# Index scores and softmax logits of a two-layer trunk: a head's high and low query parts stacked over 128 rows

## The reference, cut to what matters

```python
proj = x @ w_in + b_in            # 1024 -> q_a|k_a|v_a|g_a|q_b|k_b|v_b|g_b|q_i|k_i|w_i|r_a|r_b
head_scores = relu(einsum('bthi,bsi->bths', q_idx, k_idx))        # 8 heads of 64, one key head
index_score = einsum('bth,bths->bts', w_idx, head_scores)         # -inf where not admissible
_, sel = lax.top_k(index_score, n_select)                         # 128 keys (prompt), 80 (sample)
logits = einsum('bthd,btkd->bhtk', q, k_sel) * ATT_SCALE + bias   # 8 heads of 64, one key head
p = softmax(logits); y_b = einsum('bhtk,btkd->bthd', p, v_sel)
```

## Time and profile before

| | us |
|---|---|
| median of 3 runs | 1003.15 (1001.43 to 1004.92) |
| profiled execution | 1001.84, its span 1000.0 |
| PE busy | 970.6 (97%) |
| PE weight loads busy | 889.9 (89%) |
| DVE busy | 775.6 (78%) |
| ACT busy | 526.7 (53%) |
| POOL busy | 555.8 (56%) |
| chain that ended last | PE 77%, DVE 14%, ACT 3%, issue 3%, POOL 1% |

### The profile page before, as it was taken

The page is one execution under the profiler, slowest core; times in us unless marked ns, Lnnn a source line. Parts: engine busy times, 40 slices in busy tenths (PEclk is TensorE's granted clock), DMA queues, the critical chain, the costliest instruction groups (busy, mean ns, idle before and its releaser), DMA issues.

```text
span 1000.0 us, 18578 instructions
## 1 busy us (share of the span) xinstructions
PE 970.6 (97%) x7192; PEld 889.9 (89%) x7192; DVE 775.6 (78%) x1417; ACT 526.7 (53%) x936; POOL 555.8 (56%) x466
## 2 busy tenths in 40 slices
PE   6999998999999999999999999989999999999996
PEld 5889997788899999998888899877888999999985
DVE  7479998769997966559864899977898978656447
ACT  5564346668867454343235633476698474344320
POOL 2535555636665597676434366554465647677550
PEclk9999999999999999999999999999999999999999
DMA  7612452101112231265343135301111122231712
GB/s 218 215 48 95 160 164 90 33 13 43 54 36 82 86 111 60 85 214 185 97 161 111 44 97 167 125 16 43 44 44 43 43 85 85 86 126 43 270 46 95
DMA packets 71164, 96.51 MB, mean 97 GB/s; under 512 B 4499, under 2 KB 62341, under 8 KB 70437
## 3 DMA queue, kind: packets, MB, share of 16 engines
q1 hardware_dynamic: 67124, 83.74, 25.9%
q0 software_dynamic: 3776, 11.50, 3.2%
q10 hardware_dynamic: 176, 0.07, 0.0%
HBM read 82.09 MB, written 14.79 MB: 97 GB/s over the span
## 4 chain that ended last, share of the span: by engine, by line
PE 77%; DVE 14%; ACT 3%; issue 3%; POOL 1%; DMA 0%; DVEq 0%; ACTq 0%; POOLq 0%
PE ps L1053 21%; PE ps L676 15%; PE ps L986 10%; PE ps L1107 9%; DVE attn L1779 4%; DVE top L1776 3%; PE ps L700 3%; DVE attn L1752 3%; PE ps L901 3%; PE ps L922 2%; PE ps L961 2%; PE ps L940 2%; PE ps L724 2%; PE ps L880 2%; PE ps L1099 1%
## 5 line engine op out<-in xcount | busy, mean ns | idle before, releaser
L2200 POOL TENSOR_TENSOR w_lo<-raw,w_hi 128x512 fp32r<-128x512 f32 x71 | 97.1, 1368 | 228.8 <-ACT w_hi L1154 228.6
L676 PE MATMUL ps<-xT_hi,w_hi 128*128 128x288 f32 x480 | 143.1, 298 | 0.0
L676 PE MATMUL ps<-xT_hi,w_lo 128*128 128x288 f32 x480 | 141.4, 295 | 0.0
L676 PE MATMUL ps<-xT_lo,w_hi 128*128 128x288 f32 x480 | 141.4, 295 | 0.0
L2317 POOL TENSOR_TENSOR w_lo<-raw,w_hi 128x512 fp32r<-128x512 f32 x76 | 106.7, 1414 | 47.0 <-ACT w_hi L1511 46.6
L2201 POOL TENSOR_TENSOR w_lo<-raw,w_hi 128x512 fp32r<-128x512 f32 x71 | 103.9, 1463 | 0.0
L676 PEld LDWEIGHTS ps<-xT_hi,w_hi 128*128 128x128 f32 x480 | 90.1, 188 | 1.2 <-issue 0.6
L676 PEld LDWEIGHTS ps<-xT_lo,w_hi 128*128 128x128 f32 x480 | 90.1, 188 | 0.0
L676 PEld LDWEIGHTS ps<-xT_hi,w_lo 128*128 128x128 f32 x480 | 90.0, 188 | 0.0
L1511 ACT ACTIVATE w_hi<-raw 128x512 fp32r<-128x512 f32 x76 | 47.5, 629 | 80.6 <-PE ps L1053 49.9
L2317 POOL TENSOR_TENSOR w_lo<-w_sums,w_hi 128x512 fp32r<-128x512 f32 x48 | 73.1, 1532 | 24.9 <-ACT w_hi L1511 24.4
(11 more groups left out here) (282 smaller groups left out, 3178.8 us busy)
## 6 DMA issues: line engine op xcount, KB each, us to landing
raw<-in_w_in SPq DMA_DIRECT2D x44, 1024.0 KB, 5.2
raw<-in_w_out SPq DMA_DIRECT2D x8, 1024.0 KB, 5.3
x_kept<-x_nat SPq DMA_DIRECT2D x2, 2560.0 KB, 10.3
x_nat<-x_kept SPq DMA_DIRECT2D x2, 2560.0 KB, 10.4
raw<-in_w_proj_a SPq DMA_DIRECT2D x8, 512.0 KB, 3.5
raw<-in_w_proj_b SPq DMA_DIRECT2D x8, 512.0 KB, 4.5
x_nat<-in_x_prompt SPq DMA_DIRECT2D x4, 512.0 KB, 5.4
out<-stage POOLq DMA_DIRECT2D x8, 256.0 KB, 5.3
```

Of the source, the lines that this page charges most:

```text
L676: last = mm(out, a, b[:, HALF * half:HALF * (half + 1)], start=(k == 0 and i == 0), stop=(k == n - 1 and i == 2))
L2200: g.tensor_tensor(lo[:, 0:half, :], src[:, 0:half, :], hi[:, 0:half, :].bitcast(f32), ALU.subtract)
```

## The change: what it does

q_hi and q_lo become one array q_both[128, 2, 4, TOK]. For head hh of a pair, q_both[:, hh, m] holds the high part in the partitions where the head's queries lie and the low part in the other 64. One matmul over all 128 partitions by the high keys gives high x high plus low x high; then a matmul over the head's own 64 partitions by the low keys adds high x low. A call issues four matmuls, full, full, half, half, in place of six halves. ACT makes the high parts in two instructions of 64 partitions, and DVE and POOL the low parts in two each, which cross the partition halves. POOL also waits for the low part of a unit's weights, and for each of its two query parts in turn, before it goes on.

```diff
-        with nc.sbuf_tensor("q_hi", [128, 4, TOK], f32r) as q_hi, nc.sbuf_tensor("q_lo", [128, 4, TOK], f32r) as q_lo:
+        with nc.sbuf_tensor("q_both", [128, 2, 4, TOK], f32r) as q_both:
             pass
...
                     if s >= 4:
                         pe.wait_ge(s_relu, L * NH * N_IDX + s - 2)
-                    for i, (q, k) in enumerate(((q_hi, ki_hi), (q_hi, ki_lo), (q_lo, ki_hi))):
-                        for hh in range(2):
-                            p = slice(64 * hh, 64 * hh + 64)
-                            last = mm(ps[0:n, 4 + (s + hh) % 4, 0:nk], q[p, h // 2, t0:t0 + n], k[p, k0:k0 + nk],
-                                      start=(i == 0), stop=(i == 2))
-                            if i == 2:
-                                last.then_inc(s_is, 1)
+                    for hh in range(2):
+                        mm(ps[0:n, 4 + (s + hh) % 4, 0:nk], q_both[:, hh, h // 2, t0:t0 + n], ki_hi[:, k0:k0 + nk],
+                           start=True, stop=False, skip_group_check=True)
+                    for hh in range(2):
+                        p = slice(64 * hh, 64 * hh + 64)
+                        mm(ps[0:n, 4 + (s + hh) % 4, 0:nk], q_both[p, hh, h // 2, t0:t0 + n], ki_lo[p, k0:k0 + nk],
+                           start=False, stop=True, skip_group_check=True).then_inc(s_is, 1)
...
# logits(p): the same with kb_hi, kb_lo and s_lg; its stage waits for s_qblo at L * 8 + 8
...
-                    act_f(q_hi[:, m, at:TOK], qy[:, m if kind == "QI" else 4 + m, at:TOK], ACT.Copy).then_inc(s_qhi, 1)
+                    for hh in range(2):
+                        p = slice(64 * hh, 64 * hh + 64)
+                        last = act_f(q_both[p, hh, m, at:TOK], qy[p, m if kind == "QI" else 4 + m, at:TOK], ACT.Copy)
+                    last.then_inc(s_qhi, 1)
...
-                    v.tensor_tensor(q_lo[:, m, QI_AT:TOK], qy[:, m, QI_AT:TOK], q_hi[:, m, QI_AT:TOK].bitcast(f32),
-                                    ALU.subtract).then_inc(s_qilo, 1)
+                    for hh in range(2):
+                        p, other = slice(64 * hh, 64 * hh + 64), slice(64 - 64 * hh, 128 - 64 * hh)
+                        done = v.tensor_tensor(q_both[other, hh, m, QI_AT:TOK], qy[p, m, QI_AT:TOK],
+                                               q_both[p, hh, m, QI_AT:TOK].bitcast(f32), ALU.subtract)
+                    done.then_inc(s_qilo, 1)
...
-                    g.tensor_tensor(q_lo[:, m, :], qy[:, 4 + m, :], q_hi[:, m, :].bitcast(f32), ALU.subtract).then_inc(s_qblo, 1)
+                    pool.wait_ge(s_lo, L * T0 + u + 4)
+                    for hh in range(2):
+                        p, other = slice(64 * hh, 64 * hh + 64), slice(64 - 64 * hh, 128 - 64 * hh)
+                        pool.wait_ge(s_qblo, L * 8 + 2 * m + hh)
+                        g.tensor_tensor(q_both[other, hh, m, :], qy[p, 4 + m, :],
+                                        q_both[p, hh, m, :].bitcast(f32), ALU.subtract).then_inc(s_qblo, 1)
+                    pool.wait_ge(s_qblo, L * 8 + 2 * m + 2)
```

More of the change, by code:

```diff
@@ L834, in _ @@
                 pe.wait_ge(s_kblo, L * 2 + 2)
-                pe.wait_ge(s_qblo, L * 4 + 4)
+                pe.wait_ge(s_qblo, L * 8 + 8)
                 def logits(p):
@@ L841, in logits @@
                         pe.wait_ge(s_rm, L * N_B + 2 * p - 2)
[L842 to L848, removed]
+                    for hh in range(2):
+                        mm(ps[0:n, (2 * p + hh) % 4, 0:nk], q_both[:, hh, m, t0:t0 + n], kb_hi[:, k0:k0 + nk],
+                           start=True, stop=False, skip_group_check=True)
+                    for hh in range(2):
+                        half = slice(64 * hh, 64 * hh + 64)
+                        mm(ps[0:n, (2 * p + hh) % 4, 0:nk], q_both[half, hh, m, t0:t0 + n], kb_lo[half, k0:k0 + nk],
+                           start=False, stop=True, skip_group_check=True).then_inc(s_lg, 1)
                 logits(0)
```

## The result

The changed kernel takes 1016.45 us (median of 4 runs, 1014.33 to 1017.17) where the kernel before takes 1003.63 (4 runs, 1001.43 to 1004.92). The ratio is 1.0124, 95% interval [1.0112, 1.0136]: slower by 1.2%, and by 12.8 us between the two medians. The profiled execution took 1014.33 us, the shortest of the four, with a span 12.5 us longer than before.

A forecast was written before the change was run, and what follows sets the result against it. PE, busy 97% of the span, was taken as the bound. Terms 6.1 + 6.8 + 0.98 - 1.06 - 2.4 = +10.4 us on 1001.84 or the median 1003.15 gave 1012.3 or 1013.6; forecast 1013, range 1009 to 1016.5.

The forecast's parts named there:

- The main mechanism: PE's index and logits calls: streaming saves nothing, added passages cost 6.1 us over 16 blocks and 6.8 over 18 rounds.
- passage: PE's switch between full-height and half-height matmuls: 0.186 us going in, 0.196 coming out, 0.38 together.
- The index stage: Eight index blocks with one more passage in and out each make layer 0's stage 2.7 us longer.
- PE's two waits for relu: Index stage, 0.36 us in one layer and 0.70 in its twin: both go as PE is later, -1.06 us.
- The logits stage: Nine rounds a layer, 6.8 us over two layers, of which PE's idle time takes up 1.2 us a layer.
- The start of the index stage: ACT's second activation for m = 2 index queries stands on the path: 0.49 us later per layer, 0.98 in all.
- POOL's cover: POOL's doubled softmax query low parts stay hidden before PE takes the weights, by about 0.5 us; otherwise up to 1 us a layer.
- 1 (inner passages free): Rival: passages inside a call cost nothing and the entry from dense goes too, 996.5 us; chance 0.07.
- 2 (DVE's top-k hides the index delay): Rival: DVE's top-k is the true bound, so only +6.0 us, 1007.8; chance 0.10.
- 3: Rival: no logits take-up, short full passes load-bound, 1015.4 to 1016.8 us, 1018.8 with POOL's cover gone; chance 0.09.
- 4 (each full matmul shows its load): Rival: every full-height matmul shows its weight load, 14 us more, 1027; chance 0.04 together with 5.
- 5: Rival: a pair's half-height matmuls no longer run side by side, +12 us on top; chance 0.04 together with 4.

The follow-up runs named there:

- e2_mirror: Changed kernel, with the second call of each two in a row running its half-height pair first, full-height pair last: 1008.77 us, ratio 1.0053.
- e10_inside: Changed kernel, with the first call of each two in a row, instead of the second, running half height first: 1016.17 us, ratio 1.0120.
- e3_full: Changed kernel, with the second pass by the low keys at full height too, adding low by low: 1007.74 us, ratio 1.0044.
- e1_prep: Kernel before, with only the doubled ACT, DVE and POOL preparation and POOL's added waits, matmuls still six half-height: 1007.23 us, ratio 1.0036.
- e6_mirror_fixed: e2_mirror plus the weight cast of e4_cast and POOL's softmax query parts spread one each over eight units: 1007.92 us, ratio 1.0044.
- e7_before_cast: Kernel before, with only ACT's weight cast moved ahead of the high parts of query block m = 2: 1003.17 us, ratio 0.9997.
- e4_cast: Changed kernel, with ACT's cast of the first index stage unit's weights ahead of the high parts of m = 2: 1014.24 us, ratio 1.0109.

## Why the prediction was right

**The main mechanism was right in place and size.** The streaming saves nothing (three steps before, three after), and each block or round has one more passage in and one more out. Foretold 0.38 us, measured in the index blocks 0.41 for 512 keys, 0.40 for 384, 0.39 for 256, and 0.29 for the 64-query tiles, whose weight loads have half the columns (0.13 us a half-height load in place of 0.19). A call of 512 keys takes 0.99 us from start to start, not 1.08, because 0.10 of the passage out falls on the next call's first step. e2_mirror and e10_inside tie it to the count: 2.06 with two, 2.44 with four.

**The index stage.** Foretold 2.7 us longer in layer 0, measured 2.7; for layer 1 the same sum less 0.70 gives 2.3, measured 2.2. PE's two waits for relu are gone as expected.

**The logits stage.** Foretold 2.2 us a layer, measured 1.7 and 0.8, so this term was too large, by 1.9 us in all. PE's time in the stage without its idle time grew by 2.4 and 2.1 us, where nine rounds at 0.38 would be 3.4. The price was not the same for all tiles, as the prediction took it: rounds without a wait grew by 0.40 us at 384 keys and 0.39 at 256, but by 0.28 on the 64-query tile and 0.24 at 128 keys. That is about half of what is missing; the rest is open. PE's idle time fell from 3.37 to 2.71 us and from 4.05 to 2.71, so 0.7 and 1.3 us were taken up, against 1.2 foretold. The place was wrong in part: the 2.6 us of PE idle behind ACT are there as before, to the tenth, in every kernel of the study, so that chain moves with PE. What gave way were short waits for DVE and ACT at logits, transposes and values, in layer 1 most of all (before, it had 0.6 us on DVE in one wait and 0.3 in another where layer 0 had 0.2).

**The start of the index stage.** Foretold 0.49 a layer, measured 0.72: I took a step between two different activations for the price of one more. The activation's own 0.58 and the lost overlap with the cast are the right row.

**POOL's cover failed.** This is the step of the prediction that was wrong: "hidden, by about 0.5 us", with "up to 1 us a layer" if not. It was 0.7 and 1.6 us. The reading of layer 0 was right as far as it went: POOL ended 2.0 us before PE took the unit (95.57 and 97.61). But the weight low part slipped by 2.6 us against PE in both layers, where the prediction had 1.5. It had ACT's doubled high parts at nothing here ("the cast one unit further ahead"), and they delay the cast that POOL waits for by 0.8 us. POOL's own waits are 0.13 us before the pair and 0.29 behind it. And layer 1, which was not read, has only 1.1 us of cover in the kernel before (POOL ends at 583.77, PE takes the unit at 584.88).

**The clock was not foreseen.** The median moved by 12.8 us. The two profiled spans differ by 12.5, with 1.3 of that at the start of the program, where no instruction is changed. Without it the change costs 11.2 us.

**Luck in the number.** The sum was 10.4 against 11.2, but term by term it is further off: index stages 5.0 foretold and 4.9 measured, logits 4.4 and 2.5, start of the index stages 1.0 and 1.4, dense stretches 0 and 2.3. An excess of 1.9 and a shortfall of 2.8 nearly cancel. The median of 1016.45 is 3.4 above the forecast of 1013, of which about half is clock, and lies inside the bounds 1009 to 1016.5 by 0.05 us.

**The rivals.** 1 (inner passages free) is refuted by the block. 2 (DVE's top-k hides the index delay) too: the dense stretch and the logits' start kept all of it. 3 named a time near the result (1015.4 to 1018.8), and one of its three parts came true, POOL's cover gone. The other two did not: part of the delay was taken up in the logits, and the rounds of 128 keys grew less than the others (0.24 us). There the first full pair of a round steps at 0.06 us, the second at 0.17, and a longer run of full-height matmuls at 0.11 (e3_full); the half-height pairs of the kernel before paid 0.11 as well. 4 (each full matmul shows its load) is refuted by e3_full, whose eight full matmuls go 0.234 apart with other weights each time. 5 is refuted: each half pair is still "x2".

The prediction looked for an extra step at the transpose of the 64-query tile and found none. The entry to a 64-query block at full height shows none either:

```profile
75.43 0.29 PE L800 MATMUL ps<-xT_hi,w_lo 128*128 128x288 f32 x1
75.56 0.46 PE L779 MATMUL ps<-ki_hi,q_both 128*64 128x320 f32 x2
75.95 0.36 PE L783 MATMUL ps<-ki_lo,q_both 64*64 64x320 f32 x2
```

75.43 to 75.56 is a plain step (0.13 us), so 128*128 to 128*64 costs nothing here. The change of row height does cost, 0.19 us a passage at 512 keys, and so does the additional passage ahead of the values' products, 0.21 us a round of 384 keys (1.68 in e2_mirror, 1.47 in e1_prep).

## What to carry to other kernels

Before replacing pairs of half-height matmuls by full-height ones, count the steps and the changes of height, not the instructions: two half-height matmuls side by side already run in the time of one full-height matmul (0.233 and 0.234 us at 512 keys), and each change of height costs 0.19 us of PE here at 512 keys, 0.12 to 0.15 at the smallest tiles. If both heights are needed, order them so that runs of one height meet, across calls too, and look at what stands behind: ahead of the products by the values the passage was there too, 0.21 us a round. An added instruction on a helper engine cost its own duration plus its waits plus the overlap with its successor that was lost: 0.72 us a layer for an activation of 0.58 us on ACT, and on POOL two parts in 2.94 us with 0.13 us of waiting before and 0.29 us behind, for one part of 1.42 us. Add such costs up along the whole chain to the waiting engine: here ACT's and POOL's stood ahead of the same weight part. And read the cover in every layer, not in one.

## What the runs showed that I had not expected

PE's granted clock drops for a few microseconds in some executions, in three places: within the first 22 us (0.50 from 19 to 21 us in the changed kernel), at the start of layer 1 (0.50 from 521 to 524 us in e10_inside), and in the logits stage's first rounds, where PE has been idle for 1.6 and 0.6 us (0.50 from 167 to 170 us in e6_mirror_fixed). One of them, in e3_full: a window (clock third from the end), and two dense matmuls.

```profile
169.00:171.30 2.30, 2.30 (x12) 2.30 (x11) 1.05 (x3) 1.40 (x4) 0.49 (x1) 0.52 0.00 0
...
170.73 0.44 PE L899 MATMUL ps<-xT_lo,w_hi 128*128 128x288 f32 x1
170.97 0.41 PE L899 MATMUL ps<-xT_hi,w_lo 128*128 128x288 f32 x1
```

At a granted 0.52 the dense matmuls step at 0.24 in place of 0.131 us. Each such stretch costs 1.0 to 1.7 us. Over the runs the time goes with the mean granted clock: e1_prep took 1005.0 us at 0.998 and 1007.7 to 1009.6 at 0.994, the kernel before 1003.1 to 1003.8 at 0.997 and about 1004.7 at 0.994, the changed kernel 1014.3 at 0.996 and 1017.1 at 0.993. At equal clock (0.996: 1003.2 and 1014.3; 0.994: 1004.7 and 1015.8, one run of the changed kernel each) the change costs 11.1 us; the other 1.7 us of the median are clock.

The early drop does not go with the edit. The transposes at the start of the program step at 0.22 us (the kernel before: eight in 1.76 us from 8.58) and pass over to 0.11 (eight in 0.87 from 19.00), though the granted clock reads 1.00 from 7 to 16 us in all ten profiled executions. The drop comes in the five where they pass over at 10.8 to 11.7 us, e7_before_cast among them, and in none of the five where they do at 12.4 to 13.4 us, e10_inside among them; the 1.5 us of PE idle ahead of it are in the kernel before too. Over the whole run chance alone is not enough: beside the same kernel before, e4_cast and e10_inside had a mean granted clock of 0.994 or less in 7 of 8 runs, the kernel before and e7_before_cast in 1 of 28. So the changed forms drop more often. Why is open: the idle times ahead of the drop in the logits stage, 1.6 and 0.6 us, are the same in all kernels.
